# The first norm's root applied after the projection: x turned unscaled while weight tiles arrive, and a bias table an eighth the size

## What is computed

```python
h = rms_norm(x, pre_mix_norm[l])          # x * rsqrt(mean(x*x) + EPS) * gain
proj = h @ w_in[l]                        # 2048 x 5656
(dq, dk, dv, nq, kc, vc, ksl, vsl, kwn, vwn, g) = jnp.split(proj, offsets, axis=-1)
o_diff = diff_attention(q_d, k_d, v_d, lam, lam_init, diff_subln[l], bias_diff)
k_c = compress(kc, cmp_pos_k[l], cmp_k_w1[l], cmp_k_w2[l])   # v_c the same from vc
o_nsa = nsa_attention(q_n, k_c, v_c, k_s, v_s, k_w, v_w, gates, bias_nsa)
x = x + rms_norm(mix @ w_out[l], post_mix_norm[l])
h = rms_norm(x, pre_ffn_norm[l])
u = causal_dwconv(h @ w_up[l], conv_w[l], conv_b[l])
```

## Time and profile before

| | |
|---|---|
| median of 3 runs | 2399.59 us (2397.59 to 2401.9) |
| the profiled execution | 2398.08 us, span 2396.3 us |
| TensorE busy | 2326.6 us, 97% of the span |
| VectorE, ScalarE, GpSimd busy | 1462.1 us (61%), 1142.6 us (48%), 56.7 us (2%) |
| the largest line | L1784, 2432 matmuls, 859.8 us |
| DMA | 422.39 MB, mean 176 GB/s over the span |
| chain that ended last | PE 83%, issue 7%, DMA 4%, DVE 4%, ACT 2% |

### The profile page before, as it was taken

How to read it: one execution, slowest core, us unless ns; L and a number is a source line. 1 busy time by engine, 2 the same in 40 slices (tenths; PEclk the granted TensorE clock), 3 DMA queues, 4 the chain that set the end, 5 groups by cost and what they waited for, 6 DMA issues and landing times.

```text
span 2396.3 us, 33680 instructions
## 1 busy us (share of the span) xinstructions
PE 2326.6 (97%) x12330; PEld 1962.6 (82%) x12330; DVE 1462.1 (61%) x1893; ACT 1142.6 (48%) x1612; POOL 56.7 (2%) x81
## 2 busy tenths in 40 slices
PE   6799999999999999999999999999999999999997
PEld 5588878788888888888878888877888888888886
DVE  4355566567777446776566668866566444566544
ACT  4254455465555445555454564445444434444432
POOL 2200000000000000000010000000000000000000
PEclk9899999999999999999999999999999999999999
DMA  8974445556556566556556453354665656665652
GB/s 180 310 229 123 141 132 167 167 161 195 180 186 193 193 192 184 182 177 212 192 156 184 123 167 106 97 174 147 199 184 184 193 192 190 188 185 185 210 193 96
DMA packets 322022, 422.39 MB, mean 176 GB/s; under 512 B 13438, under 2 KB 232888, under 8 KB 321156
## 3 DMA queue, kind: packets, MB, share of 16 engines
q1 hardware_dynamic: 315968, 398.70, 53.7%
q0 software_dynamic: 5376, 20.19, 3.3%
q10 hardware_dynamic: 580, 2.20, 0.3%
HBM read 415.80 MB, written 5.25 MB: 176 GB/s over the span
## 4 chain that ended last, share of the span: by engine, by line
PE 83%; issue 7%; DMA 4%; DVE 4%; ACT 2%; POOL 0%; DVEq 0%; SPq 0%; POOLq 0%; ACTq 0%
PE PS L1784 23%; PE PS L1785 12%; PE PS L1750 7%; PE PS L1749 7%; PE PS L1748 7%; PE PS L1845 4%; PE PS L2101 3%; DMA stage<-in_w_in 2%; PE PS L1859 2%; PE PS L1861 2%; PE PS L1860 2%; PE PS L1846 2%; PE PS L2102 2%; PE PS L2112 1%; PE PS L2114 1%
## 5 line engine op out<-in xcount | busy, mean ns | idle before, releaser
L1784 PE MATMUL PS<-actT,whi 128*128 128x512 f32 x2432 | 859.8, 397 | 1.8 <-DVE wlo L1152 1.8
L1785 PE MATMUL PS<-actT,wlo 128*128 128x256 f32 x2432 | 683.4, 281 | 0.0
L1784 PEld LDWEIGHTS PS<-actT,whi 128*128 128x128 f32 x2432 | 457.2, 188 | 115.1 <-DVE wlo L1152 2.1
L1152 DVE TENSOR_TENSOR wlo<-stage,whi 128x1024 fp32r<-128x1024 f32 x298 | 362.7, 1223 | 237.0 <-ACT whi L730 236.9
L1123 DVE TENSOR_TENSOR wlo<-stage,whi 128x1024 fp32r<-128x1024 f32 x245 | 298.9, 1226 | 306.0 <-ACT whi L672 306.0
L730 ACT ACTIVATE whi<-stage 128x1024 fp32r<-128x1024 f32 x298 | 315.9, 1061 | 319.9 <-PE PS L1785 306.2
L1785 PEld LDWEIGHTS PS<-actT,wlo 128*128 128x128 f32 x2432 | 456.5, 188 | 0.1
L672 ACT ACTIVATE whi<-stage 128x1024 fp32r<-128x1024 f32 x245 | 258.3, 1059 | 349.7 <-PE PS L1750 324.9
L1750 PE MATMUL PS<-whi,gT 128*128 128x512 f32 x864 | 340.4, 394 | 0.0
L1749 PE MATMUL PS<-wlo,gT 128*128 128x512 f32 x864 | 338.7, 392 | 0.0
L1748 PE MATMUL PS<-whi,gT 128*128 128x512 f32 x864 | 335.2, 388 | 0.0
(11 more groups left out here) (332 smaller groups left out, 2787.3 us busy)
## 6 DMA issues: line engine op xcount, KB each, us to landing
stage<-in_w_up SPq DMA_DIRECT2D x304, 512.0 KB, 3.8
stage<-in_w_down SPq DMA_DIRECT2D x216, 512.0 KB, 4.4
stage<-in_w_in SPq DMA_DIRECT2D x160, 512.0 KB, 3.8
stage<-in_w_out SPq DMA_DIRECT2D x64, 512.0 KB, 3.7
DQK<-in_cmp_k_w POOLq DMA_DIRECT2D x8, 512.0 KB, 21.6
stage<-in_w_in SPq DMA_DIRECT2D x16, 256.0 KB, 3.9
DQK<-in_cmp_v_w POOLq DMA_DIRECT2D x8, 512.0 KB, 5.9
bias_by_distance<-work POOLq DMA_DIRECT2D x1, 3072.0 KB, 33.7
```

The source lines that it names most:

```text
L1152: nc.vector.tensor_tensor(wlo[:, j % SPLITS, :], stage[:, j, :], whi[:, j % SPLITS, :].bitcast(F32), ALU.subtract).then_inc(ev("lo_done"), 1)
L1784: nc.tensor.matmul(o, whi[:, j % SPLITS, at], actT[:, k, :], start=k == 0, stop=False)
L1785: last = nc.tensor.matmul(o[:, S:2 * S], wlo[:, j % SPLITS, at], actT[:, k, 0:S], start=False, stop=k == KC - 1)
```

## The change

x is no longer scaled before it is turned. SyncE issues ident and the gain vectors ahead of the weight tiles, ScalarE only x. TensorE turns x with `transpose` as soon as x is there; ScalarE and VectorE split eight chunks, then tile 0, four chunks, tile 1, four chunks, tile 2. x is squared beside tiles 4 to 7, mean and variance follow at n = 8, the diagonals at n = 9 (in `rootd`), and TensorE makes of them a row of roots on all partitions (`root_row_made`, n = 9, PS bank 4). The transposes of the other vectors move to n = 6. The root of a key's token is multiplied into keys and into kc and vc by VectorE (`in1_times_row`), into the token blocks by ScalarE's scale, and the query token's root into the scores where the bias is added (`with_bias`, now a scalar_tensor_tensor) and into the compressed scores.

The bias table is written with 16 instead of 128 copies of each row (384 KB), ahead of `inv_sqrt(1)`, and read back in eight loads of 16 partitions (256 KB each), one behind each compress load 4 to 11. The compress products move from n = 9, 11, 13, 15, 18 ... to n = 14, 16, 18 ... 44, what hangs on them by two tiles, and the last two differential heads from n = 89 and 92 to 90 and 93.

```diff
@@ -81,11 +81,11 @@
-DIFF_AT = {71 + 3 * r: r for r in range(HD)}
+DIFF_AT = {71: 0, 74: 1, 77: 2, 80: 3, 83: 4, 86: 5, 90: 6, 93: 7}
-CMP_AT = {9 + 9 * j // 4: j for j in range(16)}
-CMP_OUT = {60 + 2 * h: h for h in range(HN)}
+CMP_AT = {14 + 2 * j: j for j in range(16)}
+CMP_OUT = {62 + 2 * h: h for h in range(HN)}
...
+        ones = sb("ones", [P, P], F32, mixer1)
...
+        rootd = KSW[:, 3, :].rearrange("p (t q) -> p t q", t=TT)
...
+        def in1_rooted(k):
+
+            i = IN1_FEAT[k]
+            return i if i < 4 else 4 + (i - 9) // 2 if i >= 8 and i % 2 else None
...
+            sp.dma_start(ident[:, :], w["ident"]).then_inc(ev("ident_in"), 16)
+            for r0, nm, k in ((0, "pre_mix_norm", 16), (16, "pre_ffn_norm", 16), (32, "mix_pre_gain_2", 16),
+                              (48, "mlp_pre_gain_2", 16), (64, "attn_out_gain_2", 8), (72, "diff_subln", 1),
+                              (73, "rnn_norm_gain_2", 1)):
+                sp.dma_start(vecs[r0:r0 + k, 0, :], w[nm][0].rearrange("(r f) -> r f", f=P)).then_inc(ev("vecs_in"), 16)
             for n in range(REGION1_TILES):
...
@@ -583,6 +595,8 @@
                 row = roots.rearrange("t p -> (t p)").rearrange("(o s) -> o s", o=1)
                 pool.dma_start(root_row[:, :], row.broadcast_to((P, S))).then_inc(ev("row_in"), 16)
 
+            pool.wait_ge(ev("urow"), 2)
+            pool.dma_start(scratch, urow.rearrange("h (o k) -> h o k", o=1).broadcast_to((16, 16, SK))).then_inc(ev("scratch_out"), 16)
             inv_sqrt(1, small[:, 4:6], small[:, 2:4], 2)
...
             pool.wait_ge(ev("actlo_n1"), KC)
-            pool.wait_ge(ev("urow"), 2)
-            pool.dma_start(scratch, urow.rearrange("h (o k) -> h o k", o=1).broadcast_to((16, P, SK))).then_inc(ev("scratch_out"), 16)
             for j in range(4):
                 compress_in(j)
-            pool.wait_ge(ev("scratch_out"), 16)
-            pool.dma_start(bias[:, :, :], bass.AP(scratch.tensor, P - 1, [[SK - 1, P], [P * SK, 16], [1, S]])).then_inc(ev("bias_in"), 16)
...
             for v in range(2):
-                pool.wait_ge(ev("in1_join"), v + 1)
+                pool.wait_ge(ev("in1_rooted"), v + 1)
...
+            pool.wait_ge(ev("scratch_out"), 16)
             for j in range(4, 16):
                 compress_in(j)
+                if j < 12:
+                    at = 16 * (j - 4)
+                    pool.dma_start(bias[at:at + 16, :, :], bass.AP(scratch.tensor, P - 1 - at, [[SK - 1, 16], [16 * SK, 16], [1, S]]))\
+                        .then_inc(ev("bias_in"), 16)
...
             for t in range(TT):
                 act.dma_start(x[:, t, :], w["x"][0, t * P:(t + 1) * P, :]).then_inc(ev("x_in"), 16)
-            act.dma_start(ident[:, :], w["ident"]).then_inc(ev("ident_in"), 16)
-
...
-            first_tiles("in1")
+
+            act.wait_ge(ev("gains"), 1)
+            split_turned("n1", range(8))
+            for j in range(AHEAD):
+                act.wait_ge(ev(f"landed{j}"), 16)
+                nc.scalar.activation(whi[:, j, :], stage[:, j, :], ACT.Copy).then_inc(ev("hi_done"), 1)
+                if j < 2:
+                    split_turned("n1", range(8 + 4 * j, 12 + 4 * j))
             act.wait_ge(ev("x_in"), 32)
-            squares_of_x(0)
-            split_turned("n1")
-            act.wait_ge(ev("lam_dot"), 1)
-            nc.scalar.activation(small[:, 10:12], small[:, 8:10], ACT.Exp)
-            nc.scalar.activation(lbs[:, 16:32], lbs[:, 0:16], ACT.Exp).then_inc(ev("early_exp"), 1)
...
             def in1_tokens(k):
 
                 act.wait_ge(ev("tile_used"), used(IN1_FIRST[k] + 8))
+                act.wait_ge(ev("rstd"), 1)
                 for t in range(TT):
-                    nc.scalar.activation(in1_tok_dst(k)[:, t, :], PS[:, 2 * (k % 2) + t, 0:IN1_BLOCKS[k][2]], ACT.Copy)\
+                    nc.scalar.activation(in1_tok_dst(k)[:, t, :], PS[:, 2 * (k % 2) + t, 0:IN1_BLOCKS[k][2]], ACT.Copy,
+                                         scale=small[:, 4 + t:5 + t])\
                         .then_inc(ev("in1_tok"), 1)
...
+                if n in (98, 99):
+                    diff_high(n - 98)
...
+                if 4 <= n < 4 + 2 * TT:
+                    squares_of_x(0, (n - 4,))
+                if n == 12:
+                    act.wait_ge(ev("lam_dot"), 1)
+                    nc.scalar.activation(small[:, 10:12], small[:, 8:10], ACT.Exp)
+                    nc.scalar.activation(lbs[:, 16:32], lbs[:, 0:16], ACT.Exp).then_inc(ev("early_exp"), 1)
+                if n in (32, 48):
+                    compressed_part(n // 48)
+                if n == 50:
...
@@ -1235,12 +1253,6 @@
                 dve.wait_ge(ev("ssq"), k)
                 me(nc.vector.tensor_reduce(small[:, 0:2], parts[:, :, 4:6], AX.X, ALU.add))
                 nc.vector.tensor_scalar(small[:, 2:4], small[:, 0:2], 1.0 / D, EPS, ALU.mult, ALU.add).then_inc(ev("var"), 1)
-                if k > 1:
-                    return
-                dve.wait_ge(ev("rstd"), n)
-                for t in range(TT):
-                    nc.vector.tensor_scalar(diag[:, t, :], ident[:, :], small[:, 4 + t:5 + t], None, ALU.mult)\
-                        .then_inc(ev("diag"), 1)
 
...
@@ -1285,29 +1297,60 @@
             dve.wait_ge(ev("vecs_mm"), 1)
             me(nc.vector.tensor_copy(cols[:, 0:74], PS[:, 7, 0:74]))
             me(nc.vector.tensor_scalar(cols[:, 72:73], cols[:, 72:73], 1.0 - LAM_INIT, None, ALU.mult))
-            me(nc.vector.memset(cols[:, 74:75], 1.0))
-            me(nc.vector.tensor_copy(cols[:, C_LB:C_LB + 16], PS[:, 7, 74:90]))
-            nc.vector.tensor_copy(convT[:, :, :], PS[:, 6, :].rearrange("p (j f) -> p j f", j=4)[:, :, 0:88])
-            nc.vector.tensor_copy(posT[:, :, :], PS[:, 7, 128:192].rearrange("p (v l) -> p v l", v=2)).then_inc(ev("cols"), 1)
...
-            first_tiles("in1")
-            dve.wait_ge(ev("ident_in"), 16)
-            root_of_x(1, 1)
-            split_turned("n1")
...
+            nc.vector.memset(cols[:, 74:75], 1.0).then_inc(ev("gains"), 1)
+            split_turned("n1", range(8))
+            for j in range(AHEAD):
+                dve.wait_ge(ev("hi_done"), j + 1)
+                nc.vector.tensor_tensor(wlo[:, j, :], stage[:, j, :], whi[:, j, :].bitcast(F32), ALU.subtract).then_inc(ev("lo_done"), 1)
+                if j < 2:
+                    split_turned("n1", range(8 + 4 * j, 12 + 4 * j))
+
+            def other_vectors():
...
+            def root_diagonal():
+
+                dve.wait_ge(ev("rstd"), 1)
+                dve.wait_ge(ev("ident_in"), 16)
+                for t in range(TT):
+                    nc.vector.tensor_scalar(rootd[:, t, :], ident[:, :], small[:, 4 + t:5 + t], None, ALU.mult).then_inc(ev("diag"), 1)
+
+            def root_taken():
+
+                dve.wait_ge(ev("row_mm"), 1)
+                nc.vector.tensor_copy(root_row[:, :], PS[:, 4, 0:S]).then_inc(ev("row_set"), 1)
+
+            def in1_times_row(k):
+
+                to = in1_dst(k)
+                dve.wait_ge(ev("row_set"), 1)
+                dve.wait_ge(ev("in1_join"), IN1_FEAT[k] + 1)
+                row = root_row[:, :].rearrange("p (o s) -> p o s", o=1).broadcast_to((P, 2, S))
+                nc.vector.tensor_tensor(to, to, row, ALU.mult).then_inc(ev("in1_rooted"), 1)
...
             def with_bias(to, src, head):
 
-                nc.vector.tensor_tensor(to[:, 0:P], src[:, 0:P], bias[:, head, P:S], ALU.add)
-                return nc.vector.tensor_tensor(to[:, P:SK], src[:, P:SK], bias[:, head, :], ALU.add)
+                nc.vector.scalar_tensor_tensor(to[:, 0:P], src[:, 0:P], small[:, 4:5], bias[:, head, P:S], ALU.mult, ALU.add)
+                return nc.vector.scalar_tensor_tensor(to[:, P:SK], src[:, P:SK], small[:, 5:6], bias[:, head, :], ALU.mult, ALU.add)
...
-                    dve.wait_ge(ev("bias_in"), 16)
+                    dve.wait_ge(ev("bias_in"), 16 * 8)
...
+                    if rooted:
+                        last = nc.vector.scalar_tensor_tensor(pcs[:, t, :, 0:NC], src[:, t, :, 0:NC], small[:, 4 + t:5 + t], mask, ALU.mult, op)
...
                     branch_front(BRANCH_AT[n - 3])
                 if n - 3 in DIFF_AT:
                     diff_front(DIFF_AT[n - 3])
-                if n == 50:
+                if n == 8:
+                    root_of_x(1, 1)
+                    other_vectors()
+                if n == 9:
+                    root_diagonal()
+                    lambdas()
+                if n == 12:
+                    root_taken()
+                    in1_times_row(0)
+                    in1_times_row(1)
+                if n == 16:
+                    lambdas_done()
...
                 ended = in1_end(n - 3)
                 if ended in IN1_FEAT:
                     in1_join(ended)
+                    if ended > 1 and in1_rooted(ended) is not None:
+                        in1_times_row(ended)
...
             def turn(name, ready, n):
 
```

(50 more changed lines are left out.)

92 lines of the change are left out of this document (49 added, 43 removed).

## The result

The changed kernel takes 2385.02 us (median of 4 runs, 2382.78 to 2386.01) against 2399.9 (4 runs, 2397.59 to 2401.9): a ratio of 0.9937, 95% interval 0.9921 to 0.9953, so 14.9 us faster. 2371 was forecast, with a range up to 2385: the measured time lies on the upper end of the range. The sign and the two large gains came as told. One term was mis-sized, and some microseconds are given back in a part of the kernel that the prediction called unchanged.

What follows compares the result with a forecast made beforehand. TensorE, busy 97% of the span, was taken as the bound. Terms -15.4 - 14.7 - 1.25 - 1.4 + 1.3 (added TensorE work) + 5 - 1.9 = -28.4, from 2398.1 to 2369.7, plus 1.5 for the median: 2371 us, range 2362 to 2385.

Steps and rivals of the forecast that it cites:

- the two large gains: Tile 0 starting 15.4 us earlier, and the 14.7 us hole at n = 9 going.
- The start: TensorE's way to tile 0: it begins at 18.5 instead of 33.94, 15.4 us earlier; bounds 12 to 16.5.
- The hole at n = 9: TensorE's 14.72 us idle before its first compress product, behind the 3 MB table copy: 14.7 us gained.
- its two short waits and its clock: TensorE's waits of 0.57 and 0.68 and the clock that fell in the hole: 1.25 and 1.4 us gained.
- The bias loads' rate: Loads to 16 partitions each, taken at the table copy's 93 GB/s: 22.5 us for all eight.
- The rival at full rate: Bias loads run at full rate, so the 5 us of new waits fall away: 2366; chance 25%.
- The new wait: TensorE near tiles 28 to 36 waits for weight tiles: about 5 us, bounds 0 to 12.
- The balance of bytes against TensorE's time: From n = 14 to 36: DMA work of 59 us against TensorE's 49, 10 short, some 5 covered by lead.
- weight stream runs dry longer: Slots empty at tile 28 and the clock falls: 12 us instead of 5, and 1.4: 2380; chance 8%.
- the prediction's own sign, waits over 12: TensorE's waits near tiles 28 to 36: over 12 us would make the prediction wrong.
- Near 350: The 4.14 us wait before the differential head at n = 89: 1.9 us gained, bounds 0 and 4.1.
- The best end of the prediction's sum: Best start, no new wait and all 4.1 us near 350 gained: given as -36.9 us.

Runs made afterwards that it cites:

- spread kernel: The changed kernel with each of the eight bias loads going to every 8th partition instead of 16 neighbouring ones; 2371.55 us, ratio 0.9877.
- the second run: The changed kernel with ScalarE's copy of the first compress sum at n = 31 instead of 32; 2376.87 us, ratio 0.991.
- two pairs of profiles: Before and changed kernel, each profiled twice: 2399.9 and 2385.02 us, then unchanged once more 2397.81 and 2381.75 us.
- the heads' own run: The spread kernel with the differential heads back at 71, 74, ... 92 and the sums behind them one tile earlier; 2372.59 us, ratio 0.9883.
- the first profiles: The profiles of before and changed kernel from the first measurement, 2399.9 and 2385.02 us.

## Why the prediction was right and wrong

- **The start.** Right: -15.0 against -15.4. The gain vectors landed at 10.96 instead of 10, the first split came at 13.56 instead of 12.7, tile 0 at 18.94 instead of 18.5. One reading behind it does not hold: the granted clock of 1.00 at 26 to 28 us is no measurement, since the trace's record of the clock begins at 29.6 in that profile, where TensorE's pace picks up (12 instructions from 28 to 30, 20 from 30 to 32).
- **The hole at n = 9.** Right: gone, with its two short waits and its clock. In the spread kernel, which has no new wait, the stretch from tile 0 to the wait ahead of the head at n = 90 is 14.5 shorter than before; the sum without the new wait was -14.7 - 1.25 - 1.4 + 1.3 = -16.05. Of the 1.5 between, 1.0 are the small waits at the heads (1.51 against 0.56). The prediction had put them at nothing: "VectorE (61% busy) and ScalarE hide the added multiplies under the tiles".
- **The bias loads' rate.** Right: 93 GB/s taken from the copy, 108 measured where they ran beside tiles alone. The rival at full rate is out. But they landed 1.0 to 2.4 us behind the compress load in front of them, not 2.5 to 3: the two were under way together.
- **The new wait.** This is the step that failed: "That leaves about 5 us of new waits". It was 10.7, and 1.9 for the clock behind it. The balance of bytes against TensorE's time came near: with part of the order's share taken away, 4.45 remained. What it left out was who waits for whom at that place. ScalarE's copy for the product at n = 30 stands at n = 32, so a late stream is paid two half-size tiles further on (taking one of the two away was worth 6.3 us in the second run), and the hole is then long enough for the clock to fall. The "weight stream runs dry longer" rival had the size of this (12 and 1.4) and the turns between packets, but not the order, at 8%. By the prediction's own sign, waits over 12, it is at the border: 10.7 and 12.1 in two profiles, and over 12 in both with the clock.
- **Near 350.** Right: 1.9 forecast, 2.4 and 1.1 in two pairs of profiles, and 2.1 by the heads' own run.
- **"Nothing behind the region changes."** Wrong in effect: the same instructions took 3.3 to 5.0 us longer in two pairs of profiles, which is dips of the clock for all of the 5.0 and half of the 3.3, and 0.8 more lay outside the span.

In sum: the 14.0 us of error are, from the first profiles, 7.6 of the mis-sized wait, 5.0 behind the mark, 0.8 outside the span and 1.6 between tile 0 and the heads (1.0 of it the small waits), less 1.0 of small ones. That the time comes out at the range's upper end and not past it is partly luck: that end was made of 12 us of waits with a late start, more added work and nothing gained near 350, and of these only the waits came in full. It is luck as well that the spread kernel takes 2371.55: the 2371 holds 5 us of new waits, which that kernel hasn't, and without them the forecast was 2366. (The best end of the prediction's sum adds up to -36.7, not -36.9; the range is the same.)
